# Copying attention sums out of PSUM on ScalarE instead of VectorE, in a hybrid decoder block

## The reference

```python
p = jax.nn.softmax(s, axis=-1)
a = p[:, :, 0] - lam * p[:, :, 1]
o = jnp.einsum('bhqk,bkhd->bqhd', a.astype(v.dtype), v)
o = rmsnorm(o, g_sub) * (1.0 - lam_init)
```

## Time and profile before

| | |
|---|---|
| median of three runs | 3035.59 us (3033.98 to 3035.62) |
| the profiled execution | 3035.42 us |
| its span | 3033.3 us |
| granted TensorE clock, mean | 0.991 |
| PE busy | 2919.0 us |
| DVE busy | 1664.0 us |
| ACT busy | 1022.3 us |
| POOL busy | 975.2 us |

### The profile page before, as it was taken

The page is one execution under the profiler, slowest core; times in us unless marked ns, Lnnn a source line. Parts: engine busy times, 40 slices in busy tenths (PEclk is TensorE's granted clock), DMA queues, the critical chain, the costliest instruction groups (busy, mean ns, idle before and its releaser), DMA issues.

```text
span 3033.3 us, 39287 instructions
## 1 busy us (share of the span) xinstructions
PE 2919.0 (96%) x14082; PEld 2404.6 (79%) x14082; DVE 1664.0 (55%) x2505; ACT 1022.3 (34%) x1975; POOL 975.2 (32%) x720
## 2 busy tenths in 40 slices
PE   7999999998998999988999999999999999999998
PEld 5888888777877777777887888888887788888887
DVE  5211111389899898897556444444446544444445
ACT  4111111287786786875222111111112111111112
POOL 4220020157458365564114122212224222221222
PEclk9999999999999999999999999999999999999999
DMA  5343342733433334142752011011126101111113
GB/s 175 122 150 102 110 137 96 191 80 92 120 89 89 92 99 119 38 116 91 215 171 97 31 55 55 28 55 55 55 77 226 58 28 55 55 45 38 55 41 125
DMA packets 206424, 282.78 MB, mean 93 GB/s; under 512 B 12064, under 2 KB 136224, under 8 KB 206304
## 3 DMA queue, kind: packets, MB, share of 16 engines
q1 hardware_dynamic: 152160, 213.19, 24.3%
q10 hardware_dynamic: 53376, 67.25, 6.2%
q0 software_dynamic: 768, 0.79, 0.1%
HBM read 196.38 MB, written 84.80 MB: 93 GB/s over the span
## 4 chain that ended last, share of the span: by engine, by line
PE 47%; DVE 2%; DMA 1%; POOL 1%; issue 1%; ACT 1%; SPq 0%; DVEq 0%; ACTq 0%; POOLq 0%; PEldq 0%
PE ml_ps_y L2117 7%; PE ml_ps_y L2119 7%; PE ml_ps_y L2121 7%; PE ml_ps_u L2108 7%; PE ml_ps_u L2109 7%; PE ml_ps_u L2110 7%; PE mo_acc L1689 2%; PE mo_acc L1687 2%; PE mo_acc L1688 2%; DMA ml_dn_raw<-in_w_down_dram 1%; DMA out_dram<-ml_xres 1%; PE mo_acc L1675 0%; DVE ml_u_hi L2028 0%; DVE ml_relu L2025 0%; DVE ml_y L2036 0%
## 5 line engine op out<-in xcount | busy, mean ns | idle before, releaser
L2068 DVE TENSOR_TENSOR ml_y<-ml_y,ml_ps_y 128x512 f32<-128x512 f32 x496 | 340.7, 687 | 220.5 <-PE ml_ps_y L2121 215.3
L2117 PE MATMUL ml_ps_y<-ml_dn_hi,ml_u_hi 128*128 128x512 f32 x992 | 390.4, 394 | 11.2 <-DVE ml_y L2068 11.2
L2119 PE MATMUL ml_ps_y<-ml_dn_lo,ml_u_hi 128*128 128x512 f32 x992 | 386.8, 390 | 0.0
L2121 PE MATMUL ml_ps_y<-ml_dn_hi,ml_u_lo 128*128 128x512 f32 x992 | 386.6, 390 | 0.0
L2108 PE MATMUL ml_ps_u<-h_rows_hi,ml_up_hi 128*128 128x512 f32 x992 | 385.9, 389 | 0.0
L2109 PE MATMUL ml_ps_u<-h_rows_lo,ml_up_hi 128*128 128x512 f32 x992 | 385.9, 389 | 0.0
L2110 PE MATMUL ml_ps_u<-h_rows_hi,ml_up_lo 128*128 128x512 f32 x992 | 385.9, 389 | 0.0
L1294 DVE TENSOR_REDUCE at_nmax<-at_ps_s 128x1 f32<-128x1024 f32 (+7 forms) x384 | 347.1, 907 | 47.0 <-PE at_ps_s L1398 42.7
L2025 DVE TENSOR_TENSOR ml_relu<-ml_relu 128x512 f32<-128x512 f32 x128 | 94.5, 738 | 472.9 <-ACT ml_relu L1984 472.9
L1886 POOL TENSOR_TENSOR ml_up_lo<-ml_up_raw,ml_up_hi 128x1024 fp32r<-128x1024 f32 x62 | 162.0, 2631 | 492.7 <-ACT ml_up_hi L1956 492.7
L1893 POOL TENSOR_TENSOR ml_dn_lo<-ml_dn_raw,ml_dn_hi 128x1024 fp32r<-128x1024 f32 x62 | 148.3, 2414 | 497.2 <-ACT ml_dn_hi L1974 497.2
(11 more groups left out here) (247 smaller groups left out, 5765.3 us busy)
## 6 DMA issues: line engine op xcount, KB each, us to landing
qk<-pj_out_sb ACTq DMA_DIRECT2D x64, 512.0 KB, 2.8
ml_dn_raw<-in_w_down_dram SPq DMA_DIRECT2D x32, 1024.0 KB, 7.6
ml_up_raw<-in_w_up_dram SPq DMA_DIRECT2D x31, 1024.0 KB, 5.7
at_q<-qk SPq DMA_DIRECT2D x96, 256.0 KB
at_k<-qk SPq DMA_DIRECT2D x96, 256.0 KB
vals<-pj_out_sb ACTq DMA_DIRECT2D x32, 512.0 KB, 2.9
at_v_sb<-vals SPq DMA_DIRECT2D x32, 512.0 KB, 3.9
pj_raw<-in_w_in_dram SPq DMA_DIRECT2D x24, 512.0 KB, 4.0
```

What stands on the lines that cost most here:

```text
L2068: dve.tensor_tensor(y[:, t, cols], y[:, t, cols], ps_y[:, b % 4, :], ALU.add)\
L2117: pe.matmul(ps_y[:, b % 4, :], u_hi[:, s, f, rows], hi[:, f, cols], start=(start and f == 0), stop=False)
L2119: pe.matmul(ps_y[:, b % 4, :], u_hi[:, s, f, rows], lo[:, f, cols], start=False, stop=False)
L2121: last = pe.matmul(ps_y[:, b % 4, :], u_lo[:, s, f, rows], hi[:, f, cols], start=False, stop=(stop and f == FT - 1))
```

## The change

For differential blocks, the copy of the sums out of PSUM (times `gsub`) is issued by ACT, behind the squares, and no longer by DVE. It takes with it the wait for the store that used the same slot of `o_sb`. It waits for the block's last product (`p_used`) and no longer for `o_squared`. The planner is told the new engine, with the planned duration unchanged. Forgetting blocks are as before.

```diff
-        walk.step("o_add", b, "DVE", 0.69, end, [("o_half" if fox else "o_sq", b),
-                                                ("store", b.qb - ORING) if b.qb >= ORING else None])
+        walk.step("o_add", b, "DVE" if fox else "ACT", 0.69, end,
+                  [("o_half" if fox else "o_sq", b), ("store", b.qb - ORING) if b.qb >= ORING else None])
...
+                elif what == "o_add" and arg.kind == DIFF:
+                    q = arg.qb
+                    if q >= ORING:
+                        act.wait_ge(o_stored[q % ORING], 16 * (q // ORING))
+                    act.wait_ge(p_used, last_turn[arg.n].n + 1)
+                    act.activation(o_sb[:, q % ORING, :], ps_o[:, :], ACT.Copy, scale=gsub[:, :]).then_inc(o_free, 1)
...
-                elif what == "o_add":
+                elif what == "o_add" and arg.kind == FOX:
...
-                    if arg.kind == FOX:
-                        dve.wait_ge(o_half_ready, fox_no[n] + 1)
-                        dve.tensor_tensor(o_sb[64 * arg.s:64 * arg.s + 64, q % ORING, :], ps_o[0:64, :], o_half[:, :],
-                                          ALU.add).then_inc(o_free, 1)
-                    else:
-                        dve.wait_ge(o_squared, diff_no[n] + 1)
-                        dve.tensor_scalar(o_sb[:, q % ORING, :], ps_o[:, :], gsub[:, :], None, ALU.mult)\
-                           .then_inc(o_free, 1)
+                    dve.wait_ge(o_half_ready, fox_no[n] + 1)
+                    dve.tensor_tensor(o_sb[64 * arg.s:64 * arg.s + 64, q % ORING, :], ps_o[0:64, :], o_half[:, :],
+                                      ALU.add).then_inc(o_free, 1)
```

## The result

The changed kernel takes 3047.74 us (median of six runs, 3045.60 to 3049.27), the kernel before 3035.42 in six runs of the same comparison: a ratio of 1.0041, with a 95% interval of 1.0028 to 1.0054. It is slower by 12.3 us. The forecast was +3.2, and the result lies 1.7 us above the range for 8 in 10 (3030 to 3046). The profiled execution took 3047.69 us, at a mean granted clock of 0.987 (before 0.991).

The account below looks back on a forecast made before the run. PE, 96% busy, was taken to set the pace where most copies lie, DVE leading only between rounds. The places summed to 4 x (0 + 0.5 + 0 + 0.3) = +3.2 us, 3038.8 us; range for 8 in 10: 3030 to 3046.

Parts of the forecast that it names:

- Place A: After the block with J=1, near 746 us in round 1: ACT's idle time swallows the copy, cost 0 a round.
- Place B: After J=3, near 773 us: copy ahead of three roundings, PE's variance product later, 0.5 us a round, bounds 0 and 0.7.
- Place C: After J=2, near 793 us: idle time on ACT follows the copy, cost 0 a round, bounds -0.45 and +0.2.
- Place D: After J=0, near 800 us: exponential late behind a rounding; PE waits or only DVE and ACT run behind, 0.3 us a round.
- Moved: Step following the planner's new order of the engines' queues at the four places of each round: +3.2 us in all.
- all upper ends: Upper bounds at the four places, over four rounds: 4 x (0.6 + 0.7 + 0.2 + 0.9) = +9.6 us.
- bound: Lower bound at A: -0.6 us if the planner puts the next 1024-wide exponential ahead of the rounding at 748.03.
- The first, DVE's load decides: Rival: rounds are paced by DVE's sum of work, so all 10.6 us saved arrives: 3025.0 us, chance 0.14.
- The second, all hidden: Rival: ACT absorbs 0.6 us at each place and nothing moves: 3035.6 us, chance 0.22.
- The third, ACT's queue as a serial link at 16 places: Rival: each copy delays ACT's queue by 0.6 us, 3045.2 us, or 3049.6 with D's late exponential charged fully; chance 0.24.
- The fourth: Rival: PE's first product on ps_o waits for the late copy, 2.8 us, 3038.4; shares the forecast's chance of 0.40.
- What would show it: Signs: named orders at B and D, 0.8 us more a round, DVE idle 10 us more; otherwise stretches between rounds differing.

Follow-up runs that it names:

- the kernel that has nothing else: Kernel before with its queue order kept, the copy issued on ACT directly behind the square at all 16 places: 3041.83 us, ratio 1.0017.
- the kernel with the same order there and the full clock: Copy on ACT, order of the kernel before except steps 843 to 960 of each round, around B up to C, in the changed kernel's order: 3040.00 us.
- 60 steps ahead of B: Copy on ACT, order of the kernel before except steps 780 to 840 of each round, in the changed kernel's order: 3044.14 us, ratio 1.0030.
- one moved step: Kernel before's order, copy on ACT, with DVE's sums of block 10's tile 1 put ahead of the next maximum each round: 3041.88 us, ratio 1.0022.
- the changed kernel with the old stretch: Changed kernel with the order of the kernel before in steps 780 to 840 of each round: 3046.39 us, ratio 1.0036.
- three new plans: Kernel before with DVE's differential copy planned at 0.75 us: 3041.15 us; the changed kernel: 3047.74; the changed kernel with ACT's copy planned at 0.3 us: 3048.48.
- the short plan (0.3 us): Changed kernel with the differential copy on ACT planned at 0.3 us and not 0.69: 3048.48 us, ratio 1.0042.

## Why the prediction missed

**The sizes at the places held.** The copy on ACT: 0.69 taken, 0.68 measured. The Trainium skill (ScalarE: Activation LUTs, "What ACT_TABLE_LOAD costs") gave an estimate of 706 ns; the trace is 3% below it. The same page's rule to multiply on VectorE ("Rules for kernel authors"), for which it names speeds in bf16, is not borne out for this f32 copy: 0.68 against 0.74 us, and with the order held, the two engines make the same time. Place A 0: the kernel with the new order only behind A lost 1.8 us from A to B in four rounds, 0.45 a round, and that holds other swaps too. Place B +0.5: 0.43 to 0.45 in the kernel that has nothing else. In the changed kernel the size is right by luck: there the variance product is only 0.07 us later against the square, as the exponential had gone ahead of it, and of the 0.4 lost in rounds 2 and 3 some 0.33 lies behind the variance product (17.94 us from there to the square at C, before 17.61). Place C 0: 0. Place D +0.3: 0, though the order and the late exponential were just as worked out; of the two ways out that the text named there, it is the second, PE not waiting.

**The step that failed is "Moved".** The result lies even above the sum of all upper ends (+9.6 us), so no size of a term explains it; a term is missing. The step said that the order of every engine's work comes out of the planner, and then followed that order at four places of some 3 us each. The sum, 4 x (0 + 0.5 + 0 + 0.3), has no term for the rest of the plan. The first swap, found at A as a "bound", makes every later choice of the planner another one; between A and B, where no copy stands, it costs 7.5 us by trace, more than all four places together. The old instruction in the new order (3053.0) and the new instruction in the old order (3036.7) show from both sides that the order costs and not the engine.

**The second term that was missing is the clock.** At B, the 0.43 us of delay comes with 3.4 us at half the granted clock in some rounds, for 1.54 us. The changed kernel has two of them. In round 1 its variance product is followed by the square at C after 19.51 us, in rounds 2 and 3, at full clock, after 17.94, 1.6 less; in round 4 after 16.13, and after 14.53 in the kernel with the same order there and the full clock, again 1.6 less. So B to C is 3 x 0.4 + 2 x 1.6 = 4.4 us and not 2.0, with nothing lost in round 4 but by the clock.

**A reading that was wrong.** The text says that DVE leads only between the rounds. Its own rows have DVE above PE at A (9.52 and 9.25 of 10 us) and by a hair at D (8.96 and 8.92). The stretch behind A is the one that then lost most.

**The rivals.** The first, DVE's load decides, is refuted: without any copy nothing is gained. The second, all hidden, is what the move of the engine alone does (ratio 1.0002). The third, ACT's queue as a serial link at 16 places, has the measured time in its band, but not by its mechanism: with the copy directly behind the square at all 16 places only B pays by trace, 3.3 us from B to C (6.1 by the median). Its aside, that the new order may carry swaps further than the places, was the answer, and had no price. The fourth had no room: nobody is listed as having waited for the copy.

**What would show it.** The stretches between the rounds, which the text had told the reader to watch, stayed equal to 0.4 us; the sign came between two places of one round. "The new order, not the copy, is what counts" was right, its site was not. DVE's idle time was to grow by 10 us; it grew by 22 (12.5 more span, 9.8 less work).

**What is shown and what is argued.** Shown: the order and not the engine costs; 60 steps ahead of B are enough, put into the old order, for 9.2 us (7.4 by trace), while taken out of the changed kernel they give back 5.7 us by trace and only 1.4 of the median; one moved step, which makes the maximum of the 1024-wide scores late, costs 1.5 us a round. Argued: that most of the changed kernel's loss goes that way. Its 4.32 and 4.25 speak for it (0.45 and 0.47 us in round 1), but 0.87 lies behind the last of these exponentials, and with DVE's steps in the old order the loss is as large and, in round 1, mostly there. These scores use two halves of `ps_s` in turn, and the chain scores, maximum, exponential, scores seems to go round without slack there: PE may be 96% busy over the span, here it is 8.3 of 10 us (755 to 765, changed kernel):

```profile
755.00:760.00 5.00, 4.22 (x25) 3.38 (x25) 4.62 (x12) 3.65 (x13) 4.82 (x5) 1.00 0.00 2
760.00:765.00 5.00, 4.09 (x30) 3.60 (x29) 4.49 (x12) 3.62 (x10) 4.54 (x4) 1.00 0.29 95
```

where before it had been 9.98 (9.65 in the 10 us from 753). Not settled: which swap makes each of the three delays of the changed kernel, since one swap of DVE's alone makes most of the loss (+1.5 a round), and the other engines' swaps without DVE's make all of it too (+1.9), but together they are not 3.4. Nor is it settled why the changed kernel with the old stretch stays slow in its median.

## What to carry to other kernels

Where a planner or list scheduler fills the queues, an edit to one step is two edits, the step and a new plan; hold the order and change the step, then hold the step and change the order, before anything is said about the engine. An honest prediction gives the new plan a price of its own (three new plans here, all slower, by 5.7, 12.3 and 13.1 us of 3035) and doesn't work it out at the sites of the edit only. And ahead of an engine's loop of small depth (two score buffers here), look at what stands directly in front of each maximum in the queue: 1.1 us of sums there, once in each of four rounds, cost 6.7 us, while 10 us of copies taken away elsewhere gave nothing.

## What the runs showed of the hardware

The granted clock can fall to half for only 3.4 us. Here it fell 1.2 us after the end of PE's wait of 0.96 us at place B (changed kernel, 779.1 us), and 1.9 us after the end of one of 0.47 us (copy behind the square, 776.0 us); before, with a wait of 0.60 us, it did not fall. It does so in some rounds and not in others with the same delay: in round 1 of the kernel with the copy behind the square and not in its other three, in rounds 1 and 4 of the changed kernel, in 3 and 4 with DVE's copy in the new order, in all four with the short plan (0.3 us). It was never seen there in the kernels whose variance product was on time (before, and all kernels in which B to C did not grow). Each costs 1.5 to 1.6 us. All kernels have a stretch of 6.8 us (once 10.2) at half the clock once a round ahead of place A, from 736, 941, 1149 and 1354 us in the trace of before. Another fall of 3.4 us comes behind attention, between 1663 and 1679 us, in seven of the traces; the trace of before is not one of them. What decides between two rounds with the same delay is not shown by these runs.
